# The log decays of a Mamba-2 scan: from triangle products on TensorE to differences of running sums on GpSimd

## What is computed

```python
def segsum_exp(a):
    cs = jnp.cumsum(a, axis=-1)
    diff = cs[..., :, None] - cs[..., None, :]
    n = a.shape[-1]
    mask = jnp.tril(jnp.ones((n, n), dtype=bool))
    return jnp.exp(jnp.where(mask, diff, -jnp.inf))

# in ssd_chunked_scan: 64 heads in 8 groups, head width 64, state 128
ad = (dt * a)
decay = segsum_exp(ad)
cb = jnp.einsum('bclgn,bcsgn->bgcls', cc, bc)
y_diag = jnp.einsum('bghcls,bcsghp->bclghp', cb[:, :, None] * decay, xdt)
```

## Time and profile before

| | |
|---|---|
| median of 3 runs | 2730.33 us (2729.93 to 2732.36) |
| profiled execution, its own time | 2727.98 us |
| its span | 2726.0 us |
| TensorE busy | 2370.1 us (87%) |
| VectorE busy | 2056.4 us (75%) |
| ScalarE busy | 1007.7 us (37%) |
| GpSimd busy | 884.2 us (32%) |
| mean granted TensorE clock | 0.931 |

### The profile page before, as it was taken

The page is one execution under the profiler, slowest core; times in us unless marked ns, Lnnn a source line. Parts: engine busy times, 40 slices in busy tenths (PEclk is TensorE's granted clock), DMA queues, the critical chain, the costliest instruction groups (busy, mean ns, idle before and its releaser), DMA issues.

```text
span 2726.0 us, 38177 instructions
## 1 busy us (share of the span) xinstructions
PE 2370.1 (87%) x14404; PEld 1971.6 (72%) x14404; DVE 2056.4 (75%) x2511; ACT 1007.7 (37%) x1436; POOL 884.2 (32%) x745
## 2 busy tenths in 40 slices
PE   3799999999999999999969866666666699999994
PEld 3689999888888889999859866656556664444441
DVE  7777679788888886444576899999999786665577
ACT  2245443344444445433343322226776750000000
POOL 0000011222222220000001466656666654444354
PEclk9799999999999999999989988787787799999997
DMA  9766669666666665555646899999999879999996
GB/s 383 292 216 236 218 237 344 218 215 212 214 211 215 216 216 180 181 183 184 247 181 236 349 419 419 419 411 390 405 407 402 342 270 414 413 414 414 414 412 253
DMA packets 143723, 817.88 MB, mean 300 GB/s; under 512 B 16552, under 2 KB 19232, under 8 KB 69328
## 3 DMA queue, kind: packets, MB, share of 16 engines
q0 software_dynamic: 93200, 477.21, 44.7%
q1 hardware_dynamic: 48480, 335.95, 33.3%
q10 hardware_dynamic: 1888, 2.59, 0.3%
HBM read 811.46 MB, written 4.23 MB: 299 GB/s over the span
## 4 chain that ended last, share of the span: by engine, by line
PE 63%; DVE 24%; DMA 4%; issue 4%; ACT 3%; POOL 1%; ACTq 0%; DVEq 0%; POOLq 0%
PE aux L1133 15%; DVE rrow L2114 11%; PE ps L727 9%; PE ps L728 9%; PE ps L733 9%; PE ps L702 4%; PE ps L703 4%; PE ps L708 3%; DVE rrow_first L2114 2%; DVE ada_acc L1659 1%; PE aux L984 1%; DMA dskip<-in_D_skip 1%; DMA ada_in<-in_p_ada 1%; DMA vden<-in_p_vd 1%; DVE wlo L1590 1%
## 5 line engine op out<-in xcount | busy, mean ns | idle before, releaser
L1590 DVE TENSOR_TENSOR wlo<-raw,whi 128x2048 fp32r<-128x2048 f32 x216 | 497.2, 2303 | 312.2 <-ACT whi L1152 303.8
L1152 ACT ACTIVATE whi<-raw 128x2048 fp32r<-128x2048 f32 x216 | 412.1, 1910 | 675.1 <-PE ps L733 517.6
L2204 DVE SCALAR_TENSOR_TENSOR ps<-vrow,acc,ps 128x1024 f32<-128x1024 f32 x235 | 302.7, 1288 | 176.5 <-DMA vrow<-in_p_vg,acc 158.2
L2383 POOL DMA_INDIRECT rrow<-in_peer_u,acc x218 | 351.5, 1612 | 209.9 <-DVE dots L2114 110.5
L727 PE MATMUL ps<-h_hi,whi 128*128 128x256 f32 x1552 | 389.6, 292 | 0.2
L2114 DVE CUSTOM_DVE_ANT_0 rrow<-rrow,h 128x2048 f32<-128x2048 f32 x170 | 379.9, 2290 | 10.7 <-DMA rrow<-in_peer_u,acc 10.4
L728 PE MATMUL ps<-h_lo,whi 128*128 128x256 f32 x1552 | 377.1, 284 | 0.0
L2383 POOL DMA_INDIRECT vrow<-in_p_vg,acc x256 | 250.8, 980 | 253.9 <-DVE ps L2204 177.2
L727 PEld LDWEIGHTS ps<-h_hi,whi 128*128 128x128 f32 x1552 | 298.5, 192 | 15.5 <-issue 14.2
L728 PEld LDWEIGHTS ps<-h_lo,whi 128*128 128x128 f32 x1552 | 298.9, 193 | 5.8 <-issue 5.7
L2297 POOL DMA_DIRECT2D ada_in<-in_p_ada x128 | 69.3, 542 | 674.7 <-DVEq L1746 533.5
(11 more groups left out here) (353 smaller groups left out, 4346.6 us busy)
## 6 DMA issues: line engine op xcount, KB each, us to landing
raw<-in_p_in SPq DMA_DIRECT2D x104, 1024.0 KB, 4.9
ada_in<-in_p_ada POOLq DMA_DIRECT2D x128, 512.0 KB
vden<-in_p_vd SPq DMA_DIRECT2D x64, 1024.0 KB
ada_in<-in_p_ada SPq DMA_DIRECT2D x32, 1024.0 KB, 9.3
raw<-in_p_so SPq DMA_DIRECT2D x32, 1024.0 KB, 4.8
raw<-in_p_mo SPq DMA_DIRECT2D x16, 1024.0 KB, 6.9
raw<-in_p_bc SPq DMA_DIRECT2D x16, 1024.0 KB, 7.0
raw<-in_p_mix SPq DMA_DIRECT2D x16, 1024.0 KB, 4.8
```

The costliest lines, as they stand in the source:

```text
L1152: F(whi[:, n % 2, :, 0:cols_], raw[:, n % 4, :, 0:cols_], ACT.Copy).then_inc(hi_ready, 1)
L1590: V.tensor_tensor(wlo[:, n % 2, :, 0:cols_], raw[:, n % 4, :, 0:cols_], whi[:, n % 2, :, 0:cols_].bitcast(F32), ALU.subtract).then_inc(lo_ ...
L2204: last = V.scalar_tensor_tensor(o, row, w, o, ALU.mult, ALU.add)
L2383: return G.indirect_dma_start(out=dst, out_offset=None, in_=table, in_offset=bass.IndirectOffsetOnAxis(ap=eid_all[:, r:r + 1], axis=0))
```

## The change

The running sums of `ad` over each block of 128 tokens are made once, before the MLA output: as columns, `cum` (token on the partition, in the place of adt), and as rows, `cumT` (head on the partition). TensorE makes both from products with the upper triangle, ScalarE copies them out and stores the rows of each group in DRAM (`cum_rows`, 8 transfers of 8 KB). In each group GpSimd issues one transfer that spreads the group's 2048 row sums over all 128 partitions, into `mt` (1 MB), as soon as the previous group's y is done. It then subtracts the column sum of each token, in four pieces as before, each followed by a minimum with 0, and ScalarE takes the exponential in place. Above the diagonal the minimum leaves 0, which becomes 1 and is masked by `cbm` as before. `rad`, its products and their PSUM banks are gone. The loops on VectorE and GpSimd are written out.

```diff
+        cum = adt
-        rad = at("rad", 182 * KB, [P, 2, 4, P])
+        cumT = at("cumT", 150 * KB, [HEADS, SEQ])
...
                 mm(aux[:, 2, 0:HEADS], strict, adt[:, 0, :], start=True, stop=True)
-                mm(aux[:, 2, HEADS:2 * HEADS], upper, adt[:, 1, :], start=True, stop=True).then_inc(cum_ready, 1)
+                for b in range(BLK):
+                    mm(aux[:, 2, (b + 1) * HEADS:(b + 2) * HEADS], upper, adt[:, b, :], start=True, stop=True)
+                    last = mm(aux[0:HEADS, 3, b * P:b * P + P], adt[:, b, :], upper, start=True, stop=True)
+                last.then_inc(cum_ready, 1)
...
-                                log_decays((0, 1))
-                            if q == 3:
-                                log_decays((2, 3))
...
-                F(fromst[:, :], aux[:, 2, HEADS:2 * HEADS], ACT.Exp).then_inc(decay_ready, 1)
+                F(fromst[:, :], aux[:, 2, 2 * HEADS:3 * HEADS], ACT.Exp)
+                F(cum[:, :, :].rearrange("p b h -> p (b h)"), aux[:, 2, HEADS:3 * HEADS], ACT.Copy)
+                F(cumT[:, :], aux[0:HEADS, 3, 0:SEQ], ACT.Copy).then_inc(decay_ready, 1)
+                act.wait_ge(decay_ready, 1)
+                for g in range(GROUPS):
+                    nc.scalar.dma_start(cum_rows[g:g + 1, :].rearrange("a (b j l) -> (a j) b l", b=BLK, j=HG),
+                                        cumT[g * HG:(g + 1) * HG, :].rearrange("j (b l) -> j b l", b=BLK))\
+                        .then_inc(cum_stored, 16)
...
-                                act.wait_ge(diff_done, grp * 4 + (k + 3))
-                                F(mt[:, k // 2, 4 * (k % 2):4 * (k % 2) + 4, :].rearrange("p h l -> p (h l)"),
-                                  aux[:, 3 - k % 2, :], ACT.Exp).then_inc(decay_exp, 1)
+                                act.wait_ge(diff_ready, grp * 4 + (k + 1))
+                                m = mt[:, k // 2, 4 * (k % 2):4 * (k % 2) + 4, :]
+                                F(m, m, ACT.Exp).then_inc(decay_exp, 1)
...
-                ssd_pair(0, True)
-                with dve.Fori(1, 4) as i:
-                    S.enter(i, 2 * SSD_STEPS, 1)
-                    ssd_pair(i, False)
-                S.leave(3)
+                for i in range(4):
+                    ssd_pair(i, i == 0)
...
-                with pool.Fori(0, 4) as i:
-                    S.enter(i, 4)
+                for i in range(4):
                     for g in range(2):
                         grp = i * 2 + g
+                        if grp:
+                            pool.wait_ge(y_done, grp)
+                        G.dma_start(mt[:, :, :, :].rearrange("p b h l -> p (b h l)"),
+                                    cum_rows[ds(grp, 1), :].broadcast_to([P, BLK * HG * P])).then_inc(decay_in, 16)
                         ada2(grp + ADA_SSD, 0, True)
                         hd = i * 2 * HG + g * HG
+                        pool.wait_ge(decay_in, grp * 16 + 16)
                         for k in range(4):
                             if k == 2:
                                 ada2(grp + ADA_SSD, 1, True)
-                            pool.wait_ge(diff_done, grp * 4 + (k + 1))
-                            G.tensor_tensor(rad[:, k % 2, :, :], upper.unsqueeze(1).broadcast_to([P, 4, P]),
-                                            adt[:, k // 2, ds(hd + 4 * (k % 2), 4)].unsqueeze(2).broadcast_to([P, 4, P]),
-                                            ALU.mult).then_inc(rad_ready, 1)
+                            m = mt[:, k // 2, 4 * (k % 2):4 * (k % 2) + 4, :]
+                            S.link(G.tensor_tensor(
+                                m, m, cum[:, k // 2, ds(hd + 4 * (k % 2), 4)].unsqueeze(2).broadcast_to([P, 4, P]),
+                                ALU.subtract))
+                            G.tensor_scalar(m, m, 0.0, None, ALU.min).then_inc(diff_ready, 1)
```

More of the change, by code:

```diff
@@ L469, in build @@
         xskip_ready = sem("xskip_ready")
-        rad_ready = sem("rad_ready")
+        diff_ready = sem("diff_ready")
+        cum_stored, cum_before = c_in, 16
         cb_done = sem("cb_done")
         cb_read = sem("cb_read")
-        diff_done = sem("diff_done")
+        decay_in = sem("decay_in")
         decay_exp = sem("decay_exp")
@@ L549, in build @@
         x1_kept = nc.dram_tensor("x1_kept", (SEQ, D), F32, kind="Internal").ap()
+        cum_rows = nc.dram_tensor("cum_rows", (GROUPS, BLK * HG * P), F32, kind="Internal").ap()
         order = ["setup", "low", "att", "mla", "ssd", "g0", "so", "mix", "h2", "wq", "all"]
@@ L742, in _ @@
             pe.sem_inc(pe_used, 2)
-            pe.sem_inc(diff_done, 2)
             pe.sem_inc(acc_summed, 2)
@@ L933, in ssd_pair @@
                         grp = i * 2 + g
-                        def log_decays(ks):
-                            for k in ks:
-                                pe.wait_ge(rad_ready, grp * 4 + (k + 1))
-                                if k >= 2:
-                                    pe.wait_ge(decay_exp, grp * 4 + (k - 1))
-                                mm(aux[:, 3 - k % 2, :], strict, rad[:, k % 2, :, :].rearrange("p h l -> p (h l)"),
-                                   start=True, stop=True).then_inc(diff_done, 1)
                         for q in range(4):
@@ L972, in ssd_pair @@
                         pe.wait_ge(silu_done, grp * 5 + 5)
-                        pe.wait_ge(decay_exp, grp * 4 + 4)
                         for k, (s, l) in enumerate(((0, 0), (1, 1), (0, 1))):
@@ L2310, in _ @@
                 pool.wait_ge(decay_ready, 1)
+                pool.wait_ge(cum_stored, cum_before + 16 * GROUPS)
                 pool.wait_ge(params_in, 16 * 17)
                 pool.wait_ge(pe_used, U_SSD + 2)
-                with pool.Fori(0, 4) as i:
-                    S.enter(i, 4)
+                for i in range(4):
                     for g in range(2):
                         grp = i * 2 + g
+                        if grp:
+                            pool.wait_ge(y_done, grp)
+                        G.dma_start(mt[:, :, :, :].rearrange("p b h l -> p (b h l)"),
+                                    cum_rows[ds(grp, 1), :].broadcast_to([P, BLK * HG * P])).then_inc(decay_in, 16)
                         ada2(grp + ADA_SSD, 0, True)
                         hd = i * 2 * HG + g * HG
+                        pool.wait_ge(decay_in, grp * 16 + 16)
                         for k in range(4):
@@ L2344, in _ @@
                         ada2(grp + ADA_SSD, 3, True)
-                S.leave(4)
             if on("mix"):
```

## The result

The changed kernel takes 2742.41 us (median of 6 runs, 2738.95 to 2749.27); the kernel before, in runs between them on the same chip, 2730.13. The medians differ by 12.3 us, which is 0.45%; the ratio given with the runs, which is not the quotient of these two medians, is 1.0054, with an interval of 1.004 to 1.0068. So the change is slower, and clear of noise. The forecast was 2752, slower, with a range of 2733 to 2769. The sign and the range hold; the size is a little over half of the +21.7 us of the sum. The profiled execution took 2741.04 us, 13.1 more than that of before.

What follows compares the result with a forecast made beforehand. VectorE's chain from y to unit 6 was taken to gate TensorE once its products go. Group 0 +3.0, groups 1, 2, 3, 5, 7 +14.3, groups 4 and 6 +4.4: +21.7 on 2730.33, 2752 us; range 2733 to 2769.

Steps and rivals of the forecast that it cites:

- What bounds: Scan stage: TensorE busy 543 of 550 us, but VectorE's chain from y to unit 6, 21.64 us, as long as TensorE's.
- part 1: Scan groups: two blocks of products leave TensorE, 27.5 us in all, all won if nothing else stood behind.
- part 2: Before unit 6: it starts 0.3 us earlier at best; the other 3.1 us a group become TensorE's wait for wlo.
- Part 3: VectorE's ada updates: GpSimd's subtractions and minima delay them, unit 6 comes 1.1 us later; bounds 0.3 earlier, 1.9 later.
- Part 4: The 1 MB spread into mt each group: lands at 697 to 698, making VectorE's y 0.3 us late.
- Part 5: TensorE's 2.9 us wait before unit 6 halves its clock: 1.7 us a stretch, in 85% of groups, 1.45 us.
- Rival B: Scan stage: TensorE waits in pieces and its clock stays up; +10 us, 2740 us; chance 0.14.
- Part 6: Added products, copies and issues before the MLA output, and written-out loops: nothing; at most 3 us once, and 0 to 3.
- C: Scan stage: a GpSimd minimum delays nobody, and TensorE's clock falls; +9 us, 2740 us; chance 0.10.
- E: Wait before unit 6: TensorE takes its time back as VectorE's list shortens; up to 27.5 us, 2703 us; chance 0.07.
- D: Scan stage: neither clock loss nor delay by minima; -0.3 us in most groups, 2728 us; chance 0.09.
- F: GpSimd's spread lands after 13.9 us, its work delaying VectorE some 2 us more a group; 2768 us; chance 0.10.

Runs made afterwards that it cites:

- experiment 6: Kernel before the change, with VectorE's second pair of ada updates moved behind the split of unit 7: 2723.59 us.
- Experiments 8: Changed kernel with the early start: unit 6 begins once the convolved tiles and the weights' high part are ready, waiting for the low part later: 2718.50 us.
- 9: Changed kernel with unit 6 started early and the second pair of ada updates moved behind the split of unit 7: 2707.60 us.
- 10: Kernel before the change, with unit 6 started early and the second pair of ada updates moved behind the split of unit 7: 2725.60 us.
- experiment 7: Kernel before the change, with only the two loops over groups (VectorE's and GpSimd's) written out: 2728.38 us.
- 11: Changed kernel with unit 6 started early and the four minima of a group moved from GpSimd to ScalarE: 2707.72 us.
- 12: Changed kernel with unit 6 started early, the second pair of ada updates moved behind unit 7's split, and the minima on ScalarE: 2702.23 us.

## Why the prediction was right in sign and off in size

*What bounds, and part 1.* Right for the changed kernel. L941 is gone, and each group has TensorE idle before unit 6 with wlo as its releaser. The reading that VectorE's chain of 21.64 us already stood as long as TensorE's before the change was off: with two updates less it stays 21.64 us (experiment 6), so it was TensorE that paced it, and VectorE's own list was shorter, by the 0.6 us of part 2. Experiments 8 to 10 show that this one wait kept the 27.5 us from being won.

*Part 2, only 0.3 us a group can be taken.* Undersized. With the minima away, VectorE's chain is 21.02 us, so 0.62 us could be taken, 5 us over the scan. The wait of 0.55 us for whi 5 shrank to the 0.15 us between two instructions, and 0.2 more came off tile waits.

*Part 3, GpSimd.* The step that was mis-sized most: 1.1 us a group were forecast (with part 2 taken off) and 0.16 came. Its way of working, a GpSimd instruction that gets between VectorE's and delays them, was read right. The minimum takes 1.49 us alone, between the 1.25 taken and the 1.61 of the upper bound. I let all four updates pay, 1.5 us beyond what they paid before, and gave a minimum the full 0.88 us. The trace has 0.23 us for an update beside a minimum; the subtraction costs 0.65 us, what a multiply cost, and the first two updates' delay goes into the wait for the second tile. What reaches the chain is 0.78 us. With part 2's 0.62 taken off, unit 6 is 0.16 us later where 1.1 was forecast. My own first reading of the trace, "a minimum costs 0.23 us", was wrong in the other direction: it priced the minimum by its neighbour and not by what it displaced. The minimum itself pays: 1.80 us beside updates, 3.53 us beside a wlo that still took its 2.29 us and the multiplication by z behind it, which took 1.63 us where it took 1.22 before:

```profile
701.83 1.63 DVE L1959 TENSOR_TENSOR yg<-yg,zs 128x1024 f32<-128x1024 f32 x1
```

By the rule of the Trainium skill, "SBUF — State Buffer", section "Who interferes with whom", an update that falls on a running instruction of GpSimd would be blocked until that one ends. An estimate by this rule, with the 1.49 and 1.03 us that minimum and subtraction take alone, is 1.74 us for the fourth update, at 720.32 on the minimum of 719.82, and 1.59 us for the third, at 718.89 on the subtraction of 718.70. The 0.98 us of the fourth speaks against the rule for this one-input instruction of GpSimd; the 1.40 us of the third is nearer to it.

*Part 4, the transfer.* The landing was forecast for 697 to 698; the subtraction started at 698.60, on a trace that stands about 0.5 us later there. Right, by two errors that cancel: the transfer was issued at 692.12 and not at about 689.6, and it took 6.5 us and not 7 to 8. y was to be 0.3 us late and is 0.2. The weights are not in its queue, as part 4 has it: SyncE issues them, and only the ada tiles go through GpSimd's queue with it.

*Part 5, the clock.* A wait of 2.9 us was forecast and 2.67 came; 1.7 us for each stretch holds. I counted 85% of the groups, and it was 6 of 8 in one profile, with one double stretch, and 3 of 8 in the next. 11.6 us were in the sum, 8.7 were found in the profile compared, 7.1 net of the stretch that it lacks at the start of the stage; with the second profile in its place it would have been about 5. So the part is right in kind, and how near its size comes is luck of the execution. Rival B, the clock staying up, is what the two groups without a stretch show.

*Part 6, small parts.* Nothing, as forecast, by experiment 7 for the loops. Not tried apart: the three added products and the copies and issues before the scan. Their 3 us are there (the eight issues take 2.76 us at 387.05), but the weight copy behind them still waits 4.03 us for TensorE, and the scan starts no later than before.

*The sum.* Forecast +21.7: chains 8.0 us, clock 11.6, late y 2.1. Measured in the scan: +11.2, chains 1.1 (in group 0 the chain was forecast 1.6 late and is 0.7 early, or 0.9 late without the missing stretch), y 1.4, clock 8.7. So parts 2 and 3 carry most of the miss. Groups 4 and 6 did gain from their late tiles, 1.0 and 0.3 us, and group 5 got one of its own, 2.8 us. The period of a group was forecast at 71.5 us and is 70.5 in the mean.

*The rivals.* Two of them, B and C, gave 2740, which lies nearer to 2742.41 than the forecast's 2752, but neither describes what happened: the clock did fall, and the minima did delay the updates (0.98 us where C has 0.75). E, TensorE taking its time back, named the right place: shortening that wait gives the time back, as experiments 8, 9, 11 and 12 show, down to 25 us below before. What it lacked was an edit that isn't in this change. D didn't come. F, a late spread, didn't come in the changed kernel (8.2 us at most), but in two groups of the early start it did, for 1.1 us each and not 2.

Open: what decides in which groups the clock falls. Waits of 1.9 to 2.7 us before unit 6 gave 2 to 6 groups of 8 (5 of 8 with the shortest of them); the nine traces in which that wait is 0.7 us or less have none after 494 us, though the early start alone keeps one wait of 2.1 us before a unit 5. Seven of these nine have one at the start of the stage, between 482 and 494; neither of the two profiles of the changed kernel has it. And what made the moved updates worth 4 us in the kernel before, as far as they were.

## What to carry to other kernels

Before taking work off the engine that looks like the bound, find the next wait behind that work and ask what it really protects: here a wait for "the low part is split" stood for "the banks are free", and loosening it was worth twice the loss. Time an added instruction not by how much it slows its neighbour but by what it moves onto the critical chain. And an idle piece of 2 to 3 us on TensorE can cost more than its length (here 1.7 us more for each stretch at 0.50 behind it), so a removal that only makes it wait can lose.

## What the runs showed that I had not expected

- Products whose result nobody uses made a kernel some 10 us faster, by keeping the clock at 1.00 through the scan but for 3.4 us at its start.
- One and the same kernel, with the same waits, took 2741.04 us with 24 us of its scan at 0.50 and 2732.07 us with 10 us.
- GpSimd's minimum of 128x512 took 1.49 us alone, more than its two-input subtraction of the same size at 1.03 us, and stretched to 3.53 us beside a weight split of VectorE that lost nothing and a multiplication that lost 0.4 us.
- TensorE was busy 1.53 and 1.54 of 3.40 us at the start of the scan in two profiles; the granted clock then was 0.50 in one and 1.00 in the other.
